# Grouping 512- and 256-column products and taking high input terms first, in one long fp32 kernel

## The reference

```python
def first_block(x, ...):
    x = x + ab_mixer(rms_norm(x, ab_norm), ...)    # mLSTM in two directions, and gated spatial mixing
    x = x + square(relu(rms_norm(x, ffn_norm[0]) @ w1[0])) @ w2[0]        # 1024 -> 4096 -> 1024
    x = x + mla_mixer(rms_norm(x, c_norm), positions, ...)  # latent attention, 16 heads, rotary part
    x = x + square(relu(rms_norm(x, ffn_norm[1]) @ w1[1])) @ w2[1]
    return rms_norm(x, final_norm)

def second_block(x, ...):
    m = chunk_relpos_attention(rms_norm_2(x, g_pre_mix), w_qkv, w_o, rel_bias)
    x = x + rms_norm_2(m, g_post_mix)
    h = rms_norm_2(x, g_pre_ffn)
    return x + rms_norm_2((silu(h @ w_gate) * (h @ w_up)) @ w_down, g_post_ffn)   # 1024 -> 2816
```

## Time and profile before

| | |
|---|---|
| median of 3 runs | 895.15 us (894.41 to 895.58) |
| the profiled execution | 894.42 us, of which the span is 892.6 |
| granted TensorE clock, mean | 0.999 |
| PE busy | 877.9 us (98%), 4898 instructions |
| PEld busy | 748.0 us (84%) |
| DVE busy | 617.4 us (69%) |
| ACT busy | 441.2 us (49%) |
| POOL busy | 80.2 us (9%) |
| HBM read | 153.62 MB, 173 GB/s over the span |

### The profile page before, as it was taken

One profiled execution on the slowest core, in us unless ns is written; L12 is line 12 of the kernel. 1 busy time (PEld: TensorE's weight loads), 2 busy tenths in 40 slices (PEclk: granted clock), 3 DMA queues, 4 the chain that ended last, 5 costly groups with the idle time before them and its releaser, 6 DMA issues.

```text
span 892.6 us, 12512 instructions
## 1 busy us (share of the span) xinstructions
PE 877.9 (98%) x4898; PEld 748.0 (84%) x4898; DVE 617.4 (69%) x781; ACT 441.2 (49%) x586; POOL 80.2 (9%) x114
## 2 busy tenths in 40 slices
PE   9999999999999999999999999999999999999997
PEld 8988888888888877778888888879987888888886
DVE  6999777666666668857666666665775676676674
ACT  5795544433333577745333333374555644434432
POOL 3663110000000030011000000010000200000000
PEclk9999999999999999999999999999999999999999
DMA  9764445655554361375555555537333446555541
GB/s 296 246 211 151 147 148 200 213 190 189 188 188 170 108 206 54 100 252 196 200 190 190 191 190 197 189 125 240 131 135 95 142 144 233 189 185 191 188 142 48
DMA packets 97818, 155.87 MB, mean 175 GB/s; under 512 B 4079, under 2 KB 72332, under 8 KB 97772
## 3 DMA queue, kind: packets, MB, share of 16 engines
q1 hardware_dynamic: 95068, 149.37, 49.7%
q0 software_dynamic: 1648, 5.80, 2.1%
q10 hardware_dynamic: 1056, 0.07, 0.1%
HBM read 153.62 MB, written 1.09 MB: 173 GB/s over the span
## 4 chain that ended last, share of the span: by engine, by line
PE 87%; DVE 6%; ACT 3%; SPq 1%; issue 1%; POOL 1%; DMA 1%; DVEq 0%; POOLq 0%; ACTq 0%
PE psum L1963 20%; PE psum L1882 17%; PE psum L1884 16%; PE psum L1883 16%; PE psum L1965 10%; DVE w_lo L1231 2%; PE psum L2370 1%; ACT w_hi L755 1%; DVE h_both L1256 1%; PE psum L2400 1%; ACT h_both L784 1%; PE psum L2476 1%; SPq L517 1%; PE psum L2383 1%; PE psum L1903 1%
## 5 line engine op out<-in xcount | busy, mean ns | idle before, releaser
L1231 DVE TENSOR_TENSOR w_lo<-raw,w_hi 128x2048 fp32r<-128x2048 f32 (+3 forms) x116 | 260.3, 2251 | 93.8 <-ACT w_hi L755 50.0
L1963 PE MATMUL psum<-h_both,w_hi 128*128 128x512 f32 x784 | 278.5, 398 | 0.0
L1965 PE MATMUL psum<-h_both,w_lo 128*128 128x256 f32 x784 | 220.0, 281 | 0.0
L1963 PEld LDWEIGHTS psum<-h_both,w_hi 128*128 128x128 f32 x784 | 147.3, 188 | 36.3 <-DVE w_lo L1231 0.3
L1965 PEld LDWEIGHTS psum<-h_both,w_lo 128*128 128x128 f32 x784 | 148.0, 189 | 1.4
L755 ACT ACTIVATE w_hi<-raw 128x2048 fp32r<-128x2048 f32 (+2 forms) x71 | 129.6, 1837 | 35.6 <-PE psum L1884 33.9
L1882 PE MATMUL psum<-w_hi,g_hi 128*128 128x512 f32 x368 | 145.0, 394 | 0.7 <-DVE g_lo L1840 0.4
L1883 PE MATMUL psum<-w_lo,g_hi 128*128 128x512 f32 x368 | 143.6, 390 | 0.0
L1884 PE MATMUL psum<-w_hi,g_lo 128*128 128x512 f32 x368 | 143.5, 390 | 0.0
L773 ACT ACTIVATE w_hi<-raw 128x2048 fp32r<-128x2048 f32 x66 | 125.9, 1910 | 24.9 <-PE psum L1884 24.9
L940 ACT ACTIVATE g_hi<-g_mul 128x512 fp32r<-128x512 f32 x32 | 20.2, 633 | 171.0 <-DVE g_mul L1544 171.0
(11 more groups left out here) (275 smaller groups left out, 1082.5 us busy)
## 6 DMA issues: line engine op xcount, KB each, us to landing
raw<-in_ffn_w SPq DMA_DIRECT2D x64, 1024.0 KB, 5.3
raw<-in_w_qkv SPq DMA_DIRECT2D x12, 1024.0 KB, 5.2
raw<-in_ab_w_in SPq DMA_DIRECT2D x11, 1024.0 KB, 6.2
raw<-in_w_gate SPq DMA_DIRECT2D x11, 1024.0 KB, 5.4
raw<-in_w_up SPq DMA_DIRECT2D x11, 1024.0 KB, 5.4
raw<-in_w_down SPq DMA_DIRECT2D x11, 1024.0 KB, 5.6
raw<-in_ab_w_out SPq DMA_DIRECT2D x4, 1024.0 KB, 4.9
raw<-in_c_w_out SPq DMA_DIRECT2D x4, 1024.0 KB, 5.7
```

The lines of the kernel that those rows point to most:

```text
L1231: ins = dve.tensor_tensor(dst, src, high, ALU.subtract)
L1963: pe.matmul(bank(b + f), wh[:, k, cs], h_both[:, k, :, :].rearrange("p u s -> p (u s)"), start=k == 0, stop=False, skip_group_check=True)
L1965: ins = pe.matmul(bank(b + f)[:, 0:S], wl[:, k, cs], h_hi[:, k, :], start=False, stop=k == KB - 1, skip_group_check=True)
```

## The change

It has these parts:

- `stationary_both`: in each half f the eight 512-column matmuls come first, then the eight 256-column ones. The last up piece, which went through `stationary`, goes through `stationary_both` as well, and signals after its first half (`up_half`).
- Seams (`stationary_seam`, `moving_slice`, `latent_in`): of each portion the products with `h_hi` are issued after a wait for `h_hi` alone, those with `h_lo` after the wait for `h_lo`. The first FFN piece's sums go to bank 0 in place of 4.
- `tables` is cut in two, `rel_table` after hidden chunk 2 and `angles` after chunk 3.
- Latent attention: POOL makes `q_scale` of the first 128 tokens before the roots of the second; ACT splits piece `P_UQ + RING` ahead of `q_out(0)`; `qf_wait(7)` moves from step 9 to step 11.
- The end: the last gated chunk is made in two blocks of 128 features (256 columns) each, and the last output piece starts with the first block.
- The beginning: x and piece 0 arrive and are split, turned and multiplied in four parts each, and `warm(4)` goes. The products of piece 1 with `w_hi` are issued ahead of the constants' transposes and `spread_row`, those with `w_lo` behind. On DVE `lo(2)` moves ahead of the gate rows, `gain2` behind `lo(4)`.

The diff's core (semaphores and unchanged lines cut):

```diff
--- before.py
+++ after.py
...
+    parts = raw[:, 0, :].rearrange("p (k c) -> p k c", k=KB)
+    for c in range(4):
+        cs, ks = slice(c * D // 4, (c + 1) * D // 4), slice(c * KB // 4, (c + 1) * KB // 4)
         sp.dma_start(x[:, :, cs], x_v[:, :, cs]).then_inc(x_loaded[c], 16)
-        sp.dma_start(halves[:, ks, :], SRC[P_QK][:, ks, :]).then_inc((first_half, arrived[0])[c], 16)
+        sp.dma_start(parts[:, ks, :], SRC[P_QK][:, ks, :]).then_inc(first_part[c] if c < 3 else arrived[0], 16)
...
-    for name in ("c0", "c1", "ckv0", "cq0", "ckv1", "cq1"):
+    for name in ("c0", "c1"):
         rms(name)
     for tb in range(TB):
+        rms(f"ckv{tb}")
+        rms(f"cq{tb}")
         cq, c = JOBS[f"cq{tb}"][0], JOBS[f"c{tb}"][0]
         pool.wait_ge(rstd_ready, JOB_AT[f"cq{tb}"] + 1)
...
+    turn(T_AB, 0, 1)
+    for c in range(1, 4):
+        act.wait_ge(first_part[c] if c < 3 else arrived[0], 16)
+        cs = slice(c * PIECE // 4, (c + 1) * PIECE // 4)
+        act.activation(w_hi[:, 0, cs], raw[:, 0, cs], ACT.Copy).then_inc(hi_part if c < 3 else hi_ready, 1)
+        turn(T_AB, c, c + 1)
...
+    hi(P_UQ + RING)
     q_out(0)
-    hi(P_UQ + RING)
...
+        if isinstance(c, int) and c == GC - 2:
+            for f in range(2):
+                cs = slice(f * S, (f + 1) * S)
+                act.wait_ge(mul_out, hb + GC + f)
+                act.activation(g_hi[:, (j + 1) % 2, cs], g_mul[:, (j + 1) % 2, cs], ACT.Copy)\
+                    .then_inc(g_hi_ready, 1)
+            return
...
+    dve.wait_ge(first_part[0], 16)
+    dve.tensor_copy(w_hi[:, 0, 0:PIECE // 4], raw[:, 0, 0:PIECE // 4]).then_inc(hi_half, 1)
+    for c in range(4):
+        first_low(c)
+        turn(T_AB, c, c + 1)
...
+    lo(2)
...
-    lo(2)
-    dve.wait_ge(cols_ready, 2)
-    dve.tensor_tensor(gain2[:, :], cols[:, VEC["final_norm"]:VEC["final_norm"] + KB],
...
+    dve.wait_ge(cols_ready, 2)
+    dve.tensor_tensor(gain2[:, :], cols[:, VEC["final_norm"]:VEC["final_norm"] + KB],
+                      cols[:, VEC["g_pre_mix_2"]:VEC["g_pre_mix_2"] + KB], ALU.mult)
...
-                ins = dve.tensor_copy(g_act[:, r, :], bank(4))
+                ins = dve.tensor_copy(g_act[:, r, :], bank(0))
...
+            if between and c in (2, 3):
+                between[c - 2]()
...
-    ffn(P_FFN0, 0, T_C, ("ffn00", "ffn01"), 1, tables)
+    ffn(P_FFN0, 0, T_C, ("ffn00", "ffn01"), 1, (rel_table, angles))
...
+    def mul_block(r, f, n_up):
+        if f == 0:
+            dve.wait_ge(up_half, 1)
+        else:
+            dve.wait_ge(piece_used, n_up + 1)
+        cs = slice(f * S, (f + 1) * S)
+        dve.tensor_reduce(g_mul[:, r, cs], sums_of(6)[:, f], AX.X, ALU.add).then_inc(up_in, 1)
+        dve.wait_ge(up_in, GC - 1 + f)
+        if f == 0:
+            dve.wait_ge(act_out, GC)
+        dve.tensor_tensor(g_mul[:, r, cs], g_act[:, r, cs], g_mul[:, r, cs], ALU.mult).then_inc(mul_out, 1)
+    def lo_block(r, f):
+        cs = slice(f * S, (f + 1) * S)
+        dve.wait_ge(g_hi_ready, hb + GC + f)
+        dve.tensor_tensor(g_lo[:, r, cs], g_mul[:, r, cs], g_hi[:, r, cs], ALU.subtract)\
+            .then_inc(g_lo_ready, 1)
...
-            mul_plain(c + 1, n + 1 + 6 * i)
-        else:
-            glu_mul(c + 1, r, n + 1 + 6 * i)
+            mul_block(r, 0, n + 1 + 6 * i)
+            lo_block(r, 0)
+            mul_block(r, 1, n + 1 + 6 * i)
+            lo_block(r, 1)
+            return
...
                           start=k == 0, stop=False, skip_group_check=True)
+            for k in range(KB):
                 ins = pe.matmul(bank(b + f)[:, 0:S], wl[:, k, cs], h_hi[:, k, :],
                                 start=False, stop=k == KB - 1, skip_group_check=True)
+            if f == 0 and half_done is not None:
+                ins.then_inc(half_done, 1)
         ins.then_inc(piece_used, 1)
...
+            h_hi_wait(t, 2 * q)
+            for f in range(2):
+                for k in (2 * q, 2 * q + 1):
+                    at = bank(b)[:, f * S:(f + 1) * S]
+                    pe.matmul(at, wh[:, k, f * P:(f + 1) * P], h_hi[:, k, :], start=k == 0 and f == 0,
+                              stop=False, skip_group_check=True)
+                    pe.matmul(at, wl[:, k, f * P:(f + 1) * P], h_hi[:, k, :], start=False, stop=False,
+                              skip_group_check=True)
             h_wait(t, 2 * q)
             for f in range(2):
                 for k in (2 * q, 2 * q + 1):
-                    ins = product(bank(b)[:, f * S:(f + 1) * S],
-                                  (wh[:, k, f * P:(f + 1) * P], wl[:, k, f * P:(f + 1) * P]),
-                                  h_block(k), k == 0 and f == 0, k == KB - 1, True)
+                    ins = pe.matmul(bank(b)[:, f * S:(f + 1) * S], wh[:, k, f * P:(f + 1) * P], h_lo[:, k, :],
+                                    start=False, stop=k == KB - 1, skip_group_check=True)
...
         if t is not None and tb == 0:
-            h_wait(t, 4 * j + 2 * (i % 2))
-        for k in (2 * (i % 2), 2 * (i % 2) + 1):
-            ins = product(bank(banks[tb]), h_block(4 * (j if half is None else half) + k, tb),
-                          (wh[:, k, :], wl[:, k, :]), j == 0 and k == 0, j == 1 and k == 3)
+            h_hi_wait(t, 4 * j + ks[0])
+            for k in ks:
+                high_terms(bank(banks[tb]), h_block(4 * j + k, tb), (wh[:, k, :], wl[:, k, :]),
+                           j == 0 and k == 0)
+            h_wait(t, 4 * j + ks[0])
+            for k in ks:
+                ins = low_term(bank(banks[tb]), h_block(4 * j + k, tb), (wh[:, k, :], wl[:, k, :]),
+                               j == 1 and k == 3)
...
-        ready()
-        out_block(act_of, n_slot, 0, False, True).then_inc(acc_part, 1)
+        for k in range(2):
+            ready(k)
+            wh = w_hi[:, n_slot, :].rearrange("p (k c) -> p k c", k=2)
+            wl = w_lo[:, n_slot, :].rearrange("p (k c) -> p k c", k=2)
+            for h in range(2):
+                cs = slice(h * 512, (h + 1) * 512)
+                ins = product(bank(h), act_of(k, 0), (wh[:, k, cs], wl[:, k, cs]), False, k == 1)
+        ins.then_inc(acc_part, 1)
...
-        turn(T_AB, [(tb, k, k + 2, None) for k in (4 * c, 4 * c + 2) for tb in range(TB)])
+        turn(T_AB, [(tb, 2 * c, 2 * c + 2, None) for tb in range(TB)])
...
-    warm(4)
+    turn_first(1)
     pe.wait_ge(cols_ready, 1)
...
+    first_terms(0, (0,))
+    turn_first(2)
+    first_terms(1, (0,))
+    first_terms(0, (1, 2))
+    turn_first(3)
+    first_terms(2, (0,))
+    first_terms(1, (1, 2))
+    first_terms(3, (0,))
+    first_terms(2, (1, 2))
+    first_terms(3, (1, 2)).then_inc(piece_used, 1)
...
-    pe.wait_ge(ws_loaded, 16)
-    for g in range(B_G):
-        pe.transpose(bank(1)[:, g * P:(g + 1) * P], ws_raw[:, g, :], ident[:, :])
-    pe.wait_ge(vecs_loaded, 16 * (len(VEC) - 1))
-    pe.transpose(bank(3)[:, 0:VECS], vecs[:, :], ident[0:VECS, 0:VECS]).then_inc(vecs_turned, 1)
+    def turn_constants():
...
+        for g in range(B_G):
+            pe.transpose(bank(1)[:, g * P:(g + 1) * P], ws_raw[:, g, :], ident[:, :])
+        pe.wait_ge(vecs_loaded, 16 * (len(VEC) - 1))
+        pe.transpose(bank(3)[:, 0:VECS], vecs[:, :], ident[0:VECS, 0:VECS]).then_inc(vecs_turned, 1)
...
+    pe.wait_ge(hi_half, 2)
+    for f in range(2):
+        for k in range(KB):
+            at = bank(QK_ORDER[1])[:, f * S:(f + 1) * S]
+            pe.matmul(at, wh[:, k, f * P:(f + 1) * P], h_hi[:, k, :], start=f == 0 and k == 0, stop=False,
+                      skip_group_check=True)
+            pe.matmul(at, wh[:, k, f * P:(f + 1) * P], h_lo[:, k, :], start=False, stop=False,
+                      skip_group_check=True)
+    turn_constants()
     spread_row(0, 6)
     split(P_QK + 1)
-    stationary((P_QK + 1) % RING, T_AB, QK_ORDER[1])
+    for f in range(2):
+        for k in range(KB):
+            ins = pe.matmul(bank(QK_ORDER[1])[:, f * S:(f + 1) * S], wl[:, k, f * P:(f + 1) * P], h_hi[:, k, :],
+                            start=False, stop=k == KB - 1, skip_group_check=True)
...
         split(first)
-        stationary_seam(first % RING, t, 4, x_at)
+        stationary_seam(first % RING, t, 0, x_at)
...
+                h_hi_wait(T_C, ks[0])
+                for k in ks:
+                    for b, c0, c1 in outs:
+                        high_terms(bank(b)[:, 0:c1 - c0], h_block(k, 0),
+                                   (wh[:, k - k0, c0:c1], wl[:, k - k0, c0:c1]), k == 0)
+                h_wait(T_C, ks[0])
+                for k in ks:
+                    for b, c0, c1 in outs:
+                        ins = low_term(bank(b)[:, 0:c1 - c0], h_block(k, 0),
...
             qf_wait(6)
+        if i == 11:
             qf_wait(7)
...
-        if isinstance(c, int) and c == GC - 1:
-            stationary((n0 + 1) % RING, T_GLU, 6)
-        else:
-            stationary_both((n0 + 1) % RING, 6)
```

(43 more changed lines are left out.)

88 lines of the change are left out of this document (42 added, 46 removed).

## The result

The changed kernel takes 888.91 us (median of 4 runs, 888.42 to 889.77), against 895.12 for the one before: a ratio of 0.9932, 95% interval 0.9915 to 0.995. The forecast was 889.0. The profiled execution took 889.77, with a span of 887.9 and a mean granted clock of 0.995, where all others of this kernel have 0.997 and the kernel before 0.999. The forecast's sum was worked out for the profiled execution, 888.3, and that one took 1.5 us more. That the medians agree to 0.1 us is luck: terms that are off cancel, so what follows takes the sum apart.

The account below looks back on a forecast made before the run. PE was taken as the bound almost everywhere (87% of the span). Terms of 9.4 us gained and 3.3 lost gave 6.1 less than the profiled 894.42, 888.3, or 889.0 against the median; range 885.3 to 892.5.

Parts of the forecast that it names:

- end: Last gated chunk and output piece: made in two blocks, the kernel ends no sooner; 0.4 us lost.
- beginning: Start of the kernel: spread_row comes later, so PE stands still 4.3 us before piece 3; 2.9 us lost.
- grouping: Input pieces in stationary_both: a pair costs 4.6 ns less with sizes grouped, counted for 7 of 8; 3.2 us gained.
- FFN0 and FFN1 seams: First piece of each FFN: h_hi products first remove two PE waits for h_lo; 0.84 us gained at each.
- tables: PE's wait for w_lo at 141.45, behind DVE's tables block: cutting it in two gains 0.5 us.
- latent attention, two waits: PE's waits at 330.21 and 339.30: earlier split and q_scale gain 1.4 and 0.5 us.
- attention step 9: PE's wait at 362.76 for the last turned queries: moving it to step 11 gains 1.0 us.
- order-neutral rival: Input pieces: the 4.6 ns belong to the matmuls' kinds, not size changes; 3.2 us not gained, 892.2; chance 0.10.
- the clock: Beginning: the 4.3 us standstill lets the granted clock fall to 1.2 GHz, some 3 us paid twice; 892; chance 0.01.
- the start costs nothing: Beginning: lo of piece 3 needn't wait for the scans, so 2.9 us comes back; 886.1; chance 0.16.
- The released waits come back: Latent part and attention: the 2.9 us gained there is waited for a few pieces on; 891.9; chance 0.15.
- Weight loads show: Grouped 256-column matmuls: 189 ns weight loads no longer hide, costing 47 us; 939; chance 0.04.

Follow-up runs that it names:

- e9: The changed kernel with all of the beginning's edits undone; 884.65 us, ratio 0.9887 to the kernel before.
- e1: The kernel before with only stationary_both grouped, eight 512-column matmuls of a half, then eight 256-column ones; 891.30 us, ratio 0.9955.
- e2: The kernel before with groups of two in stationary_both, two 512-column matmuls, then two 256-column ones, four times a half; 890.84 us, ratio 0.9951.
- e12: The changed kernel with POOL's order of before, q_scale after all six roots, ACT's early split kept; 889.82 us, ratio 0.9947.
- e5: The changed kernel with 16 idle matmuls of 128 columns put ahead of the wait for piece 3; 887.36 us, ratio 0.9915.
- e3: The changed kernel with the constants' transposes and spread_row put back ahead of piece 1's products with w_hi; 885.24 us, ratio 0.9892.

## Why the prediction was right

**What bounds the kernel.** PE, nearly everywhere: the gains below, read from the traces, add up to 10.8 us, less 0.8 for the end, and e9, with all but the beginning, is 9.9 us faster. The same terms in the forecast give 9.4 - 0.4 = 9.0.

Each step, with what PE's starts in the two traces show, as the growth of the distance between like instructions:

| term | forecast | measured |
|---|---|---|
| grouping, 49 pieces | 3.2 gained | 3.9 (e1; 0.081 a piece) |
| last up piece | 0.2 | 0.2 |
| FFN0 and FFN1 seams | 0.84 each | 1.0, 0.9 |
| seams before the attentions | 0.48 each | 0.48, 0.49 |
| tables | 0.5 | 0.6 |
| latent attention, two waits | 1.4, 0.5 | 1.5, 0.6 |
| attention step 9 | 1.0 | 1.1 |
| end | 0.4 lost | 0.8 lost |
| beginning | 2.9 lost | 5.5 in the trace, 4.0 to 4.3 in the medians |

Taking each wait as its bracket and 0.16 us worked: no wait term is off by more than 0.2. The seams, the tables and attention step 9 have no run of their own; their sizes are readings of the two traces. Grouping: the single prices held (226 to 230 and 119 to 120 ns in the groups), and the size was 0.7 short, inside the bounds given. Some 0.45 of that is the eighth that was taken off for the ends of the groups, 784/8 x 4.6 ns, and the rest lies within the rounding of the single prices. The reason given with the term, a price for each change of size, is refuted by e2. The order-neutral rival is refuted by e1: the same matmuls take 5.640 us a piece in one order and 5.559 in the other.

The estimate of 325 ns a pair in any order, worked out in the prediction from the Trainium skill (TensorE: Matmul & The Clock Gate; the 2.5 ns stand in its section "Wait — 56ns, not 53.3ns?"), disagrees with this kernel both in size, 352.5 and 347.4 ns measured, and in having no term for the order.

**The step that failed** is "The beginning": it summed the standstill alone, 2.9 us. The standstill is right to 0.1 us at each of its marks (`spread_row`, PE's stop at 29.6, piece 3, and so 33.82 - 31.04 = 2.8 us). But the rival "the clock" was given 0.01, and it is what happened. The granted clock fell to 1.2 GHz in the standstill, and the 28 distances after it were of some 213 ns in place of 120: 2.7 us more in the profiled execution, and 1.4 in e12's, where the low clock lasted less long. e5 shows the cause: with PE kept busy by idle products the clock stays, and in the trace the 2.7 us are back. The term measures 5.5 us in the trace (2.8 and 2.7), and 4.0 to 4.3 in the medians, which 2.8 and 1.4 would give. It had been in view: of the same kind is the earlier trace rows, where the engine starts at the low level. The Trainium skill (TensorE: Matmul & The Clock Gate, section "What's actually happening") says that the gate throttles by default and activity opens it; by that rule a standstill of several us was worth far more than one in a hundred. This case's profile agrees: 0.50 behind the standstill, 1.00 in e5, where idle products fill it. The underrated gains elsewhere, 0.9 us by e9, brought most of the loss back. A shorter stretch at the low clock in the other runs would bring the rest; it is argued from their mean clocks (0.997 against 0.995) and not shown. That the sum came to 889 was luck.

**The end.** PE goes on with the first block 2.1 us after `w_lo`, about as soon as with the undivided chunk before (2.2), and the second 1.97 later; PE has 1.37 us of products between, so it waits again, 0.5 lost. The reduction of half width cost 0.68, the forecast 0.61.

**The rival "the start costs nothing"** is out: e3 moves only the constants' transposes and `spread_row`, and takes 3.7 us off. **"The released waits come back"** is out in latent attention and the attentions; one of the kind is there in the last FFN, 0.19 for `w_lo` at 730.89, where before nothing was recorded. **"Weight loads show"** is out: loads of 190 ns are recorded under products 120 ns apart, in groups of eight too.
